# Second attention: transposes of the probabilities taken from TensorE to VectorE and DMAs, and an opening with an early table and early matmuls

## The reference, cut to what matters

```
def attend_blocks(q, k_all, v_all):            # q (B,S,16,128), k/v (B,T,4,128), T = 512 keys
    s = jnp.einsum('bqkgd,btkd->bkgqt', qblk, k_all) * 128 ** -0.5
    p = jax.nn.softmax(s, axis=-1)
    return jnp.einsum('bkgqt,btkd->bqkgd', p, v_all)
```

## Time and profile before

| | |
|---|---|
| median of three runs | 3192.54 us (3190.09 to 3192.74) |
| profiled execution | 3192.07 us |
| its span | 3190.3 us |
| TensorE matmuls busy | 3159.6 us, 99% |
| VectorE, ScalarE, GpSimd busy | 65%, 46%, 15% |
| DMA engines over the stretch of the second attention | 36% |

### The profile page before, as it was taken

The page is one execution under the profiler, slowest core; times in us unless marked ns, Lnnn a source line. Parts: engine busy times, 40 slices in busy tenths (PEclk is TensorE's granted clock), DMA queues, the critical chain, the costliest instruction groups (busy, mean ns, idle before and its releaser), DMA issues.

```text
span 3190.3 us, 42014 instructions
## 1 busy us (share of the span) xinstructions
PE 3159.6 (99%) x15288; PEld 2608.1 (82%) x15288; DVE 2082.9 (65%) x2507; ACT 1478.0 (46%) x1834; POOL 490.7 (15%) x743
## 2 busy tenths in 40 slices
PE   8999999999999999999999999999999999999998
PEld 7888888888777888888988878888878877888886
DVE  6777775556886567777876554665666755445556
ACT  5444444444337444444444445544455554544443
POOL 1111116947660001111100000000000100000000
PEclk9999999999999999999999999999999999999999
DMA  7888886556453678888876655546866643665654
GB/s 246 278 287 284 286 258 198 195 191 198 139 157 101 207 229 285 284 281 282 286 248 218 195 185 177 176 142 184 166 139 191 187 130 100 182 200 179 212 184 152
DMA packets 317405, 655.37 MB, mean 205 GB/s; under 512 B 20872, under 2 KB 29328, under 8 KB 316608
## 3 DMA queue, kind: packets, MB, share of 16 engines
q1 hardware_dynamic: 290480, 555.91, 53.9%
q0 software_dynamic: 26768, 97.35, 12.5%
HBM read 647.93 MB, written 2.10 MB: 204 GB/s over the span
## 4 chain that ended last, share of the span: by engine, by line
PE 97%; DVE 1%; ACT 0%; issue 0%; POOL 0%; DMA 0%; SPq 0%; DVEq 0%; ACTq 0%; POOLq 0%
PE acc L279 24%; PE acc L281 24%; PE acc L280 24%; PE acc L990 2%; PE pst L990 2%; PE acc L992 2%; PE pst L992 2%; PE pst L991 2%; PE acc L991 2%; PE pst L2742 1%; PE pst L2724 1%; PE pst L2434 1%; PE pst L804 1%; PE pst L2436 0%; PE pst L1617 0%; PE pst L2732 0%
## 5 line engine op out<-in xcount | busy, mean ns | idle before, releaser
L247 DVE TENSOR_TENSOR w_lo<-w_raw,w_hi 128x1024 fp32r<-128x1024 f32 x1060 | 1317.3, 1247 | 908.7 <-ACT w_hi L240 899.7
L240 ACT ACTIVATE w_hi<-w_raw 128x1024 fp32r<-128x1024 f32 x1060 | 1122.7, 1061 | 1424.9 <-PE acc L281 1126.2
L279 PE MATMUL acc<-w_hi,act_hi 128*128 128x512 f32 (+1 forms) x3360 | 1322.5, 394 | 4.1 <-DVE w_lo L247 4.0
L281 PE MATMUL acc<-w_hi,act_lo 128*128 128x512 f32 (+1 forms) x3360 | 1303.3, 388 | 0.0
L280 PE MATMUL acc<-w_lo,act_hi 128*128 128x512 f32 (+1 forms) x3360 | 1301.7, 387 | 0.0
L279 PEld LDWEIGHTS acc<-w_hi,act_hi 128*128 128x128 f32 x3360 | 631.5, 188 | 132.3 <-issue 9.0
L281 PEld LDWEIGHTS acc<-w_hi,act_lo 128*128 128x128 f32 x3360 | 631.0, 188 | 128.8
L280 PEld LDWEIGHTS acc<-w_lo,act_hi 128*128 128x128 f32 x3360 | 631.9, 188 | 122.5 <-issue 0.5
L699 POOL DMA_DIRECT2D mod_ring<-in_w_mod x160 | 115.8, 724 | 933.8 <-DVE pst L715 771.9
L715 DVE SCALAR_TENSOR_TENSOR pst<-mod_ring,c_act,pst 128x512 f32<-128x512 f32 x300 | 226.0, 753 | 6.3 <-DMA mod_ring<-in_w_mod 0.6
L990 PE MATMUL acc<-w_hi,g_hi 128*128 128x512 f32 x344 | 134.7, 392 | 0.0
(11 more groups left out here) (464 smaller groups left out, 2401.8 us busy)
## 6 DMA issues: line engine op xcount, KB each, us to landing
w_raw<-in_w_in SPq DMA_DIRECT2D x400, 512.0 KB, 3.7
w_raw<-in_ffn_w_down SPq DMA_DIRECT2D x168, 512.0 KB, 4.0
w_raw<-in_ffn_w_gate SPq DMA_DIRECT2D x160, 512.0 KB, 4.7
w_raw<-in_ffn_w_up SPq DMA_DIRECT2D x160, 512.0 KB, 5.3
mod_ring<-in_w_mod POOLq DMA_DIRECT2D x160, 512.0 KB, 5.5
w_raw<-in_w_out SPq DMA_DIRECT2D x64, 512.0 KB, 4.2
w_raw<-in_w_branch_a SPq DMA_DIRECT2D x32, 512.0 KB, 4.0
w_raw<-in_w_branch_b SPq DMA_DIRECT2D x32, 512.0 KB, 4.6
```

Source lines behind the costliest of these rows:

```text
L240: act.activation(weight_tiles(s)[0], w_raw[:, s % SLOTS, :], ACT.Copy).then_inc(w_hi_done, 1)
L247: dve.tensor_tensor(lo, w_raw[:, s % SLOTS, :], hi.bitcast(F32), ALU.subtract).then_inc(w_lo_done, 1)
L279: pe.matmul(o, xh, wh, start=k == 0, stop=False)
L281: mm = pe.matmul(o, xl, wh, start=False, stop=k == 2 * nch - 1)
```

## The change

1. The second attention has no transposes on TensorE and no copy on ScalarE. ScalarE writes the exponential back to its own PSUM bank (three banks in rotation, u%3). VectorE transposes 128x512 in 32x32 blocks from the bank to `a2_blocks` in SBUF. The blocks are put in their places by DMAs from SBUF to SBUF: sixteen for each head, each of 32 KB in runs of 128 bytes; eight are issued by SyncE (`attention2_move_sp`, behind loads of later chunks) and eight by GpSimd. The products with the values come at step u+5 in place of u+3, the fetch at u+6, and there are 38 steps in place of 36.
2. VectorE's step s does the block transpose of half head s-1 first, then the fetch of s-6, then the maximum of s.
3. The loads of `x_ga` and `x_zb` are written out and not looped.
4. At the opening, the table (Silu's) is loaded ahead of the first wait; chunk 0 is rounded in two halves, with a semaphore of its own for the first; and TensorE issues eight matmuls of 128x128 by the identity twice (`warm_pe`): once ahead of the tokens' arrival, once behind the first transposes. Their results are overwritten.
5. Some semaphores are merged: `mod_done` with `mod_added`, `d_ready` with `bs_ready`, `row_ready` with `att_consts` (that wait is moved ahead), `ones_set` and `bb_prod` with VectorE's step counter.

```
+        def round_first_chunk(act):
+            act.wait_ge(w_raw_ready[0], 16)
+            act.activation(w_hi[:, 0, 0:BLK], w_raw[:, 0, 0:BLK], ACT.Copy).then_inc(first_hi, 1)
+            act.activation(w_hi[:, 0, BLK:2 * BLK], w_raw[:, 0, BLK:2 * BLK], ACT.Copy).then_inc(w_hi_done, 1)
+        def warm_pe(pe, n):
+            for _ in range(n):
+                pe.matmul(acc[:, 1, 1, 0:P], ident[:], ident[:], start=True, stop=True)
...
                     rows_turn_pe(self.pe, self.use, p)
+                if self.loaded is not None and j == 0:
+                    warm_pe(self.pe, 8)
                 self.pe.wait_ge(tt_lo, ROW_PAIRS * self.use + j + 1)
...
-        ATT2_STEPS = NQ + 4
+        A2_LAG = 5
+        ATT2_STEPS = NQ + A2_LAG + 1
+        A2_MOVED = 16 * 8
         def attention2_step_pe(pe, s):
...
             if s < NQ:
-                if s >= 2:
-                    pe.wait_ge(a2_probs, s - 1)
+                if s >= 3:
+                    pe.wait_ge(a2_turned, s - 2)
                 head, h = s // 2, s % 2
-                pe.matmul(pst[:, s % 2, :], qb_t[:, head, h * P:(h + 1) * P], keys_t[:, head // 4, :],
+                pe.matmul(pst[:, s % 3, :], qb_t[:, head, h * P:(h + 1) * P], keys_t[:, head // 4, :],
                           start=True, stop=True).then_inc(a2_scores, 1)
-            u = s - 2
-            if 0 <= u < NQ:
-                pe.wait_ge(a2_probs, u + 1)
-                if u >= 1:
-                    pe.wait_ge(a2_copied, u)
-                for b in range(4):
-                    mm = pe.transpose(pst[:, 2, b * P:(b + 1) * P], probs2[:, u % 2, b * P:(b + 1) * P], ident[:])
-                mm.then_inc(a2_turned, 1)
-            u = s - 3
+            u = s - A2_LAG
             if 0 <= u < NQ:
-                head = u // 2
-                pe.wait_ge(a2_copied, u + 1)
+                head, h = u // 2, u % 2
+                for queue in range(2):
+                    pe.wait_ge(a2_moved[queue][head % 2], A2_MOVED * (head // 2 + 1))
                 if u >= 1:
                     pe.wait_ge(a2_fetched, u)
...
+                dve.wait_ge(a2_probs, u + 1)
+                for queue in range(2) if head >= 2 else ():
+                    dve.wait_ge(a2_moved[queue][head % 2], A2_MOVED * (head // 2))
+                dve.transpose(a2_blocks[:, head % 2, :, h, :, :].rearrange("p d b c -> p b d c"),
+                              pst[:, u % 3, :].rearrange("p (b d c) -> p b d c", b=4, d=4)).then_inc(a2_turned, 1)
+            u = s - A2_LAG - 1
...
+        def attention2_move(eng, head, queue):
+            eng.wait_ge(a2_turned, 2 * head + 2)
+            if head >= 2:
+                eng.wait_ge(a2_out, 2 * head - 2)
+            for g in (2 * queue, 2 * queue + 1):
+                for d in range(4):
+                    eng.dma_start(a2_keys[head % 2][32 * d:32 * d + 32, :, 32 * g:32 * g + 32],
+                                  a2_blocks[32 * g:32 * g + 32, head % 2, d, :, :, :].rearrange("p h b c -> p (h b) c")
+                                  ).then_inc(a2_moved[queue][head % 2], 16)
+        def attention2_move_sp(sp, n):
+            for head in range(NH_B):
+                if -(-(2 * head + 2) * 32 // ATT2_STEPS) + 8 == n:
+                    attention2_move(sp, head, 0)
```

More of the change, by code:

```diff
@@ L200, in build @@
         mod_ready = [sem("mod_ready0"), sem("mod_ready1")]
-        mod_used, mod_turned, mod_parted, mod_summed, mod_added, mod_done = (
-            sem("mod_" + n) for n in ("used", "turned", "parted", "summed", "added", "done"))
+        mod_used, mod_turned, mod_parted, mod_summed, mod_added = (
+            sem("mod_" + n) for n in ("used", "turned", "parted", "summed", "added"))
         eye_ready = sem("eye_ready")
@@ L247, in rest_chunk, with rest_first_chunk @@
             dve.tensor_tensor(lo, w_raw[:, s % SLOTS, :], hi.bitcast(F32), ALU.subtract).then_inc(w_lo_done, 1)
+        def round_first_chunk(act):
+            act.wait_ge(w_raw_ready[0], 16)
+            act.activation(w_hi[:, 0, 0:BLK], w_raw[:, 0, 0:BLK], ACT.Copy).then_inc(first_hi, 1)
+            act.activation(w_hi[:, 0, BLK:2 * BLK], w_raw[:, 0, BLK:2 * BLK], ACT.Copy).then_inc(w_hi_done, 1)
+        def rest_first_chunk(dve):
+            for half, (done, lo_done) in enumerate(((first_hi, first_lo), (w_hi_done, w_lo_done))):
+                cs = slice(half * BLK, (half + 1) * BLK)
+                dve.wait_ge(done, 1)
+                dve.tensor_tensor(w_lo[:, 0, cs], w_raw[:, 0, cs], w_hi[:, 0, cs].bitcast(F32), ALU.subtract).then_inc(lo_done, 1)
+        def warm_pe(pe, n):
+            for _ in range(n):
+                pe.matmul(acc[:, 1, 1, 0:P], ident[:], ident[:], start=True, stop=True)
         def split_ahead(eng, s0, k, i, nch, first=LEAD, last=None):
@@ L268, in block_product @@
                     turning.before_chunk(j)
-                pe.wait_ge(w_lo_done, c0 + j + 1)
+                opening = isinstance(c0, int) and c0 + j == 0
+                pe.wait_ge(first_lo if opening else w_lo_done, c0 + j + 1)
                 slot = (s0 + j) % SLOTS
                 for kk in range(2):
+                    if opening and kk:
+                        pe.wait_ge(w_lo_done, 1)
                     k = 2 * j + kk
@@ L1065, in pairs, with stream_sp @@
                     body(i, s0, i * (2 * nch) + s0, i + p0)
-        def stream_sp(sp, name, w, col0, first_k=0):
+        def stream_sp(sp, name, w, col0, first_k=0, behind=None):
             nch = job(name)[2]
@@ L1074, in body @@
                                    c + nch * m + j)
-            pairs(sp, name, body, unrolled=bool(first_k))
+                        if behind is not None:
+                            behind(sp, nch * (2 * i + m) + j)
+            pairs(sp, name, body, unrolled=bool(first_k) or behind is not None)
         def stream_pe(pe, name, between=None, turning=None, halves=False, operand=None, flip=0, first_k=0):
@@ L1943, in build @@
         assert r.o <= top2
-        probs2 = at("probs2", [P, 2, BLK], offset=area5)
-        probs2_t = at("probs2_t", [P, 2, BLK], offset=area5 + 4 * 2 * NKV_B * HD_B)
+        a2_blocks = at("a2_blocks", [P, 2, 4, 2, 4, 32], offset=area5)
+        a2_keys = [at(f"a2_keys{n}", [P, 2 * 4, P], offset=o) for n, o in enumerate((-(-r.o // 64) * 64, top2))]
+        assert -(-r.o // 64) * 64 + 4096 <= top2
         ob_hi = at("ob_hi", [P, KT, SEQ], F32R, offset=area3)
@@ L1973, in build @@
             sem("a2_" + n) for n in ("scores", "max", "probs", "turned", "out", "fetched"))
-        a2_copied = sem("a2_copied")
+        a2_moved = [[sem(f"a2_moved_{q}{n}") for n in range(2)] for q in ("sp", "pool")]
         gr_turned, gr_copied, gr_spread = sem("gr_turned"), sem("gr_copied"), sem("gr_spread")
@@ L2741, in attention2_step_pe @@
                 for b in range(4):
-                    mm = pe.matmul(pst[:, 3, 0:HD_B], probs2_t[:, u % 2, b * P:(b + 1) * P],
+                    mm = pe.matmul(pst[:, 3, 0:HD_B], a2_keys[head % 2][:, 4 * h + b, :],
                                    vals[:, b, kv * HD_B:(kv + 1) * HD_B], start=b == 0, stop=b == 3)
@@ L2808, in fetch @@
                 o, g = (x[:, :, bass.ds(blk * BLK, BLK)] for x in (sg_a, sg_b))
-                dve.tensor_tensor(g, g, acc[:, m, :, :], M_).then_inc(bb_prod, 1)
-                dve.wait_ge(bb_prod, blk + 1)
+                steps.did(dve.tensor_tensor(g, g, acc[:, m, :, :], M_))
+                steps.settle()
                 dve.tensor_tensor(o, o, g, A_).then_inc(fetched[m], 1)
@@ L2903, in _ @@
                     (n, KB0 + BLK * b) for n, b in (("x_o", 2), ("x_q", 10), ("x_z", 6), ("x_ga", 18), ("x_zb", 14), ("x_gb", 22))):
-                stream_sp(sp, name, win2, col)
+                stream_sp(sp, name, win2, col, behind={
+                    "x_ga": attention2_move_sp, "x_zb": lambda sp, n: attention2_move_sp(sp, n + 32)}.get(name))
             stream_sp(sp, "ba", A["w_branch_a_2"], 0)
@@ L2917, in _ @@
                 rows_hi_act(act, 0, j)
-                round_chunk(act, j)
+                if j:
+                    round_chunk(act, j)
+                else:
+                    round_first_chunk(act)
             ffn_act(act, "ffn1", 0)
@@ L2983, in _ @@
                 rows_lo_dve(dve, 0, j)
-                rest_chunk(dve, j)
+                if j:
+                    rest_chunk(dve, j)
+                else:
+                    rest_first_chunk(dve)
             ffn_dve(dve, "ffn1", 0, x_ready)
@@ L3004, in _ @@
             dve.memset(va[:, :, :, DV_A:VA], 1.0)
-            dve.memset(ones_row[:], 1.0).then_inc(ones_set, 1)
-            dve.wait_ge(ones_set, 1)
+            steps.did(dve.memset(ones_row[:], 1.0))
+            steps.settle()
             stream_split(dve, "ctx_v", between=spread(cv_step_dve, dve, XV_STEPS, "ctx_v"))
@@ L3117, in _ @@
                     q_gain_pool(pool, g, h)
+            for head in range(NH_B):
+                attention2_move(pool, head, 1)
```

44 lines of the change are left out of this document (19 added, 25 removed).

## The result

The changed kernel takes 3197.93 us, median of 16 runs (3194.07 to 3201.86), beside 3190.08 us for the kernel before on the same chip (16 runs, 3189.62 to 3192.96). The ratio is 1.0021, 95% interval 1.0014 to 1.0028: slower, where I had forecast 9.1 us less (3183, range 3175 to 3197). The profiled span is 3200.1 us in place of 3190.3. Over the 16 executions the time goes with the mean granted clock, from 0.999 at 3194.07 to 0.996 at 3201.86.

What follows compares the result with a forecast made beforehand. TensorE, with 97% of the chain of waits, was taken to bound the kernel. Transposes -13.9, calls with two steps +7.6, moves +1.1 and opening -3.9 sum to -9.1 us on 3192.07: forecast 3183, range 3175 to 3197.

Steps and rivals of the forecast that it cites:

- What bounds the kernel: Whole kernel: TensorE holds 97% of the chain of waits, so an edit counts by TensorE time added, taken or waited.
- The transposes: Second attention: taking 32 half heads' transposes, 0.43 to 0.44 us each, from TensorE gives -13.9 us.
- The calls with two steps: Second attention: in five such calls TensorE's values wait 1.5 us for VectorE's fetch behind its block transpose, +7.6 us.
- Ordinary steps hide it: Second attention, VectorE: the added 0.72 us block transpose is hidden, with about 3.4 us of work in a 4.5 us period.
- The opening: Kernel start: chunk 0 starts 1.9 us earlier and runs at the fast level, 2.06 more; sum -3.9 us.
- The moves: Second attention: DMAs of block-transposed data land in time except head 14's, +1.1 us, bounds 0 and +8.
- lagging call: Second attention: a call where SyncE's rounding lags a chunk, its moves ready 4.5 us later, just reaching 14.6.
- Moves late, but not by packets: Second attention: landing beside weight traffic takes 4 to 5 us on SyncE's queue, +4 to +8 us, 3189; chance 0.17.
- The slower side: Second attention: small packets fill the DMA engines, setting the pace from 23 ns; at 33 ns 3222 us; chance 0.15.
- The last line of that rival: Second attention: a DMA of 256 short runs holds GpSimd or SyncE 1 us, not 0.5; 4 us a head, some 3215.
- The chances: Whole kernel against no change: faster by over 0.2% 0.62, within 0.23, slower 0.15.

## Why the prediction was wrong

- **What bounds the kernel** held. The transposes were TensorE's own time: with no long wait in the way, TensorE's busy time falls from 155.7 to between 142.2 and 142.9, by 12.8 to 13.5 us of the 13.9.
- **The calls with two steps** held: five stalls of 1.3 us, 6.5 us where 7.6 was forecast, in the place and by the order that was counted. Moving the fetch ahead of the block transpose takes them away.
- **The opening** held: 3.5 us for 3.9. Table and halves bring chunk 0 forward by 2.0 (1.9 forecast). The extra matmuls shorten it by 1.7 (4.57 to 2.83; 2.06 forecast) and hold it up by 0.45, which was not in the sum.
- **"Ordinary steps hide it", of the block transpose, is the step that failed.** I counted VectorE's own time, 3.4 us in 4.5, and not the wait that stands in front of the instruction. The diff has it in plain sight: for head 2 and later, VectorE waits on `a2_moved` before it writes a block buffer again. The prediction asked of the moves only when TensorE wants them, at step 2h+5. VectorE wants the buffer back at the same step, but at its start, ahead of the fetch that TensorE needs. In the example above TensorE's values of that step could have started at 2606.15 + 0.86 = 2607.01. From the start of the block transpose to those values it is 1.3 us (2608.06 to 2609.36), so the moves had to land by 2605.7, 1.3 us earlier than the deadline I used. VectorE was ready for them from 2604.72 on, the end of its `w_lo`. They landed by 2608.06: 1.0 us late for the values themselves, 2.35 us late by the way over VectorE.
- **The moves** were mis-sized, and with them the late start. In the example SyncE's moves began 9.7 us behind the start of step 2h+2 (2591.08 to 2600.73), where I had 8.0 for a lagging call (3.5 and 4.5). The eight issues took 5.2 us, at 0.61 each and some 0.65 with the step between two, where I had 0.37 to 0.6. Some 2 us more passed to the landing. That is 17.0 where the values were wanted at 15.9. I wrote that the lagging calls "just reach" the deadline of 14.6, and my upper end was added up wrong: 3.5 + 4.8 + 3.7 is 12.0 and not 11, so 16.5 in a lagging call, 1.9 past it. With no slack by my own count, that was the place to put a price. The heads behind the four long waits (2, 5, 8, 11) and head 14 are those whose step 2h+2 lies in a call with two steps. The long waits cost TensorE 8.5 us on the fetch (15.0 less 6.5), and it waited 2.6 us for head 14's moves, where I had 1.1.
- **The clock** behind the long waits was not in the sum at all. TensorE's busy time is 7.3 us above that of the kernel with early moves, 6.2 of it in the four slow stretches.
- **The account.** The span came out 9.8 us longer and not 9.1 shorter, 18.9 us apart. The long waits are 8.5 of it, the busy time above 142.9 is 7.3, the transposes gave 1.1 less, head 14 took 1.5 more, and the opening gave 0.4 less with the 1.4 lost behind it; the stalls in the double calls took 1.1 less. That makes 19.1.
- **The rivals.** "Moves late, but not by packets" was the right mechanism with the wrong price, +4 to +8 where it was +15 (3197.9 to 3182.6), and its place was VectorE and not only TensorE. The slower side was to come from packets. They cost what the bounds said: SyncE's queue 54.2% of 167.8 us, less 35.2% of 155.68 before, by 16 and by 34861 packets, is 16.6 ns for a packet, nearly all of them of 128 bytes (12 taken, 10 to 33 bounds). The same sum gives 13.9 ns in the changed kernel with early moves and 17.9 in the one with half the issues. By my sum they would have set the pace from 23 on. The DMA share of 0.68 lies in the forecast 65 to 75%. The kernel with long runs shows that they were not it. The last line of that rival (an issue that holds SyncE 1 us would look alike) was nearer: at 0.65, with the late place, it was enough. Its price does not follow, though: 4 us a head are 64 us in 16 heads, and not the 32 that give 3215.
- **The chances.** Slower had 0.15, on packets alone. The wait on the two block buffers was a slower side of its own, and the diff showed it.

Had the moves been one load earlier, the forecast would have stood: 3182.6 measured with the one edit, 3183.0 forecast. That it is so close is partly luck: there the stalls and head 14 cost 2.0 us less than forecast, and transposes and opening gave 1.5 less.

## What to carry to other kernels

When a step is cost "at nothing, hidden", list every wait in front of the instruction, also those for a buffer to come free, and give each its deadline: the earliest engine that wants the buffer sets it, not the consumer of the data. Where a producer's slack comes out at zero, treat it as late and price the chain behind it, with the slow clock that can follow an idle TensorE (behind four of the five waits of 1.9 us and more in the changed kernel). Work that rides on a queue of loads is late by its place in the stream; try the place one load earlier before adding buffers.

## What the runs showed of the hardware

- An issue of a 32 KB move between two places of SBUF takes 0.61 us on SyncE and 0.58 on GpSimd with 256 runs of 128 bytes, 0.59 and 0.50 with 32 runs of 1 KB, and 0.64 and 0.68 with 64 KB in 512 runs. On SyncE it is nearly a fixed cost of each issue, so few large moves are better than many small ones. It isn't the move's shape alone: a weight load issued right behind eight moves took 0.60 us too (2605.95 above), where the median of these loads is 0.37. What sets it was not settled. The Trainium skill's page "DMA: Bandwidth & Descriptors", section "Anatomy of one DMA — SWDGE (gpsimd) path", says of GpSimd's path that many descriptors can be emitted before the added cost shows. The trace agrees in part: on GpSimd sixteen times the runs (and twice the bytes) cost 185 ns on top of 498, on SyncE 51 ns on top of 591.
- A packet of 128 bytes took 16.6 ns of a DMA engine by SyncE's queue in the changed kernel, and 13.9 to 17.9 ns in the others with short runs, about as much as one of 256 bytes from the gains. It is a mean beside the weights' traffic, whose packets are taken to cost what they did before. The estimate of 8 ns that the prediction worked out from the Trainium skill's "DMA: Bandwidth & Descriptors" ("Why small descriptors are slow (HBM only)") is about half of it; the measurement decides. GpSimd's moves of the same shape appear as only 4096 packets with 4.20 MB, 1 KB in the mean. By the size classes the stretch has 2101 more packets of 2 KB and above than before, and none between 512 bytes and 2 KB, so they are rather some 2048 of 2 KB and as many small ones. They took 13.3% of 167.8 us by 16 and by 4096, which is 87 ns a packet or 11 ns a run of 128 bytes:

```profile
DMA packets 47474, 25.02 MB, mean 149 GB/s; under 512 B 37368, under 2 KB 37368, under 8 KB 47463
...
q1 hardware_dynamic: 43367, 20.68, 54.2%
q0 software_dynamic: 4096, 4.20, 13.3%
```

- The granted clock does not follow the length of a wait alone. In the changed kernel one wait of 2.19 us (to 2609.36) and those of 2.12, 1.95 and 2.59 us were followed by matmuls at the slow level; another of 2.19 us (to 2668.89) and the five of 1.3 us were not. With the third block buffer none of the waits, up to 2.5 us, was followed by a slow stretch. What else decides was not settled.
- A stretch in which TensorE has only short pauses from 3.0 us on brings chunk 0, at 10.34, to the fast level. Without the extra matmuls TensorE idled 1.8 us ahead of chunk 0, most of its matmuls stand at 0.43 us, and the first at the fast level comes at 13.76.
